# A GpSimd release, six VectorE instructions and a sum moved in the routing step of a mixture of experts

## The reference

```python
probs = softmax(t @ router_w + router_b)
grouped = probs.reshape(-1, N_GROUPS, EXPERTS_PER_GROUP)
group_score = sum(top_k(grouped, 2)[0], axis=-1)
g_sel = argmax(group_score)
top_v, top_i = top_k(where(in_group(g_sel), probs, -1.0), 2)
gates = top_v / sum(top_v, axis=-1)
for e in range(16):
    gu = t @ w_gu[e]
    h = silu(gu[:, :256]) * gu[:, 256:]
    out = out + combine[:, e:e + 1] * (h @ w_down[e])
x = layer_norm(ALPHA * x + out)
```

## Time and profile before

| | us |
|---|---|
| median of three runs | 872.21 (871.42 to 874.04) |
| the profiled execution | 871.15 |
| its span in the profile | 869.4 |
| TensorE busy | 846.3 (97%) |
| VectorE busy | 568.5 (65%) |
| ScalarE busy | 428.1 (49%) |
| GpSimd busy | 128.9 (15%) |

### The profile page before, as it was taken

How to read it: one execution, slowest core, us unless ns; L and a number is a source line. 1 busy time by engine, 2 the same in 40 slices (tenths; PEclk the granted TensorE clock), 3 DMA queues, 4 the chain that set the end, 5 groups by cost and what they waited for, 6 DMA issues and landing times.

```text
span 869.4 us, 10034 instructions
## 1 busy us (share of the span) xinstructions
PE 846.3 (97%) x4026; PEld 684.2 (79%) x4026; DVE 568.5 (65%) x716; ACT 428.1 (49%) x429; POOL 128.9 (15%) x126
## 2 busy tenths in 40 slices
PE   8999999999999999999998999999999999999986
PEld 6888888888888578888864888888888678888853
DVE  4532434456756789999966625425666699999947
ACT  4433222353522388888864131122314388888860
POOL 2400000010400222243220000000000223323210
PEclk9999999999999999999999999999999999999999
DMA  9993313112459399999969432220247599999863
GB/s 344 354 351 97 98 49 96 49 49 98 125 203 374 104 392 346 362 353 345 321 236 383 171 97 98 97 96 1 97 174 311 189 390 349 357 328 355 310 224 146
DMA packets 80835, 193.86 MB, mean 223 GB/s; under 512 B 8249, under 2 KB 8437, under 8 KB 80656
## 3 DMA queue, kind: packets, MB, share of 16 engines
q1 hardware_dynamic: 67344, 159.46, 51.1%
q0 software_dynamic: 13440, 33.69, 10.6%
HBM read 178.95 MB, written 30.43 MB: 241 GB/s over the span
## 4 chain that ended last, share of the span: by engine, by line
PE 88%; DVE 5%; DMA 4%; issue 1%; ACT 1%; SPq 0%; POOL 0%; ACTq 0%; POOLq 0%
PE ps L497 61%; PE ps L878 8%; PE ps L573 3%; PE ps L821 3%; PE ps L647 2%; PE ps L632 2%; DMA expert_out<-arena,rows_of 1%; DMA arena<-expert_out 1%; PE ps L849 1%; PE ps L556 1%; DVE w_lo L1377 1%; PE ps L582 1%; PE ps L736 1%; PE ps L729 1%; PE ps L864 1%
## 5 line engine op out<-in xcount | busy, mean ns | idle before, releaser
L1377 DVE TENSOR_TENSOR w_lo<-arena,w_hi 128x2048 fp32r<-128x2048 f32 x100 | 229.5, 2296 | 125.1 <-ACT w_hi L1062 123.4
L1062 ACT ACTIVATE w_hi<-arena 128x2048 fp32r<-128x2048 f32 x100 | 191.5, 1915 | 158.2 <-PE ps L497 150.6
L497 PE MATMUL ps<-w_hi,xt_hi 128*128 128x512 f32 x480 | 192.4, 401 | 0.0
L497 PE MATMUL ps<-w_hi,xt_lo 128*128 128x512 f32 x480 | 187.4, 390 | 0.0
L497 PE MATMUL ps<-w_lo,xt_hi 128*128 128x512 f32 x480 | 187.1, 390 | 0.0
L497 PE MATMUL ps<-xt_hi,w_hi 128*128 128x512 f32 (+1 forms) x336 | 125.7, 374 | 1.9 <-DVE xt_lo L1385 1.9
L497 PE MATMUL ps<-xt_hi,w_lo 128*128 128x512 f32 (+1 forms) x336 | 124.0, 369 | 0.0
L497 PE MATMUL ps<-xt_lo,w_hi 128*128 128x512 f32 (+1 forms) x336 | 123.9, 369 | 0.0
L497 PEld LDWEIGHTS ps<-w_hi,xt_lo 128*128 128x128 f32 x480 | 90.1, 188 | 19.3
L497 PEld LDWEIGHTS ps<-w_lo,xt_hi 128*128 128x128 f32 x480 | 90.3, 188 | 17.7
L497 PEld LDWEIGHTS ps<-w_hi,xt_hi 128*128 128x128 f32 x480 | 90.2, 188 | 17.5
(11 more groups left out here) (245 smaller groups left out, 1038.1 us busy)
## 6 DMA issues: line engine op xcount, KB each, us to landing
arena<-in_moe_w_gu SPq DMA_DIRECT2D x64, 1024.0 KB, 16.6
arena<-in_moe_w_down SPq DMA_DIRECT2D x32, 1024.0 KB, 17.6
arena<-in_mlstm_w_in SPq DMA_DIRECT2D x16, 1024.0 KB, 6.6
arena<-in_conv_w_in SPq DMA_DIRECT2D x12, 1024.0 KB, 11.6
expert_out<-ln_b POOLq DMA_DIRECT2D x8, 1024.0 KB, 13.8
arena<-expert_out SPq DMA_DIRECT2D x16, 512.0 KB, 7.5
arena<-in_mlstm_w_out SPq DMA_DIRECT2D x4, 1024.0 KB, 5.0
x_of_experts<-arena SPq DMA_DIRECT2D x8, 512.0 KB, 10.3
```

Source lines behind the costliest of these rows:

```text
L497: ins = pe.matmul(out, a, b, start=first and n == 0, stop=last and n == 2)
L1062: act.activation(w_hi[:, parity, :], raw(slot), ACT.Copy).then_inc(s_hi, 1)
L1377: dve.tensor_tensor(w_lo[:, parity, :], raw(slot), w_hi[:, parity, :].bitcast(F32), ALU.subtract).then_inc(s_lo, 1)
```

## The change

Three moves, each made in both layers. On GpSimd the release `s_gi` is raised between the first gather and the second. On VectorE the six instructions of the shares leave `choose` and stand in `experts` between the remainders of the first expert's two weight parts. The sum over places, with its wait for TensorE's second table, stands behind the second of these remainders. TensorE's, ScalarE's and SyncE's programs stay as they are.

```diff
@@ choose
                 step_done(dve.tensor_copy(last_token[:, :], ps[:, 7, 2 * (E - 1):2 * (E - 1) + 1]))
 
+            def shares_by_expert():
+
                 do(dve.tensor_tensor(r_one[:, :], top_value[:, 0, :], top_value[:, 1, :], ALU.add))
                 do(dve.reciprocal(r_one[:, :], r_one[:, :]))
                 do(dve.tensor_tensor(gate_of[:, :, :], top_value[:, :, :],
...
                 by_expert(gates, shares).then_inc(s_gv, 1)
+
+            def slot_gates(layer):
                 dve.wait_ge(s_gm, layer + 1)
                 dve.tensor_reduce(gate_slot[:, :], ps[:, 7, 2 * E:4 * E].rearrange("p (e c) -> p e c", c=2), AX.X,
                                   ALU.add).then_inc(s_gs, 1)
@@ experts, VectorE
                 dve.wait_ge(s_gi, layer + 1)
                 units(0, 0, 0)
+                shares_by_expert()
                 units(0, 0, 1)
+                slot_gates(layer)
                 gathered_lo(0, 0)
@@ experts, GpSimd
-                for e in range(2):
-                    gather(e, e)
+                gather(0, 0)
                 pool.engine_nop().then_inc(s_gi, 1)
+                gather(1, 1)
                 norm_weights(1 + 2 * layer, ln2_g[layer], ln2_b[layer])
```

More of the change, by code:

```diff
@@ L266, in trunk @@
         s_rc = sem("router_weights_centred")
-        s_gi = sem("first_gathers_issued")
+        s_gi = sem("first_gather_issued")
         s_xr = sem("x_tile_ready")
```

## The result

The changed kernel takes 888.63 us, the median of four runs (884.28 to 890.99), against 871.82 us of the kernel before in the same measurement: 1.0174 times as long, with an interval of 1.0129 to 1.0218. Measured again beside the first experiments it took 887.25 us against 871.96, ratio 1.0186 (1.0162 to 1.021). So it is 15 to 17 us slower. I had said slower by 11 to 12, 883.0 us, with a range up to 885.3: the direction and the wait are as forecast, the size is not, because the price of TensorE's lower clock came out at twice what I had put in.

A forecast was written before the change was run, and what follows sets the result against it. The prediction took TensorE, busy 97% of 869.4 us, as the bound. 871.15 us plus 8.50 for the wait and 3.0 for the clock gave 882.65, 883.7 on the median; it said 883.0, range 879.2 to 885.3.

The forecast's parts named there:

- What is late and what is exact: Around the routing stages: the gates have no slack, within 0.2 us; the weight remainders and first gather's landing end no wait.
- Release and order on VectorE: First remainder starts 1.32 us sooner per layer; shares follow it, so gates are ready at 299.58 and 685.42 us.
- What stands behind the wait: On TensorE's queue, table, fillers, transposes and experts' products start 4.30 and 4.20 us later: 8.50 us in all.
- What comes back: In the expert stage, earlier remainders are hidden and worth nothing; up to 2.4 us possible, taken as 0.
- Second gather: Running beside a remainder, it takes likely 1.0 us, at worst 3112 ns; its transposes stay covered, so 0 added.
- TensorE's clock: After idling about 4.2 us per layer TensorE returns at half rate: 1.5 us per layer, 3.0 us for both.
- Rival (a): TensorE's delay without a full double clock fall: none gives 879.7 to 880.7 us, one up to 882.2; chance 0.36.
- (b): VectorE and GpSimd slow each other, by a stretched remainder or later release: 884.3 to 885.6 us; chance 0.07.
- (c): Not slower, as transfers set the expert stage's pace and loads are released sooner: 868.5 to 872.2 us; chance 0.04.
- (d): Release comes when the gather is issued, not worked off; remainder 1.1 us sooner per layer: 877.5 to 881 us; chance 0.05.

The follow-up runs named there:

- shares_first: The changed kernel with the six instructions of the shares back ahead of VectorE's wait, early release and later sum kept: 871.81 us, ratio 0.9994 to the kernel before.
- old_release: The changed kernel with GpSimd's release back behind both gathers, the shares still between the remainders: 891.35 us, ratio 1.0211 to the kernel before.
- fill_wait: The changed kernel with five more calls of fillers ahead of TensorE's wait for the shares: 880.92 us, ratio 1.0115 to the kernel before.
- fill_moved: The changed kernel with five more filler calls ahead of TensorE's wait and the four behind the table taken out: 874.55 us, ratio 1.0019 to the kernel before.
- wide_first: The changed kernel with the four filler calls moved between TensorE's wait and the gates' table: 888.18 us, then 885.03 us measured again.
- table_late: The changed kernel with TensorE's wait and gates' table moved behind the first tile's transposes, six filler calls ahead of these: 872.09 us, ratio 0.9973 to the kernel before.

## Why the prediction was right and where it failed

- What is late and what is exact: right. The gates had no slack and became what TensorE waits for; the remainders were not late, and starting them sooner is worth nothing (shares_first).
- Release and order on VectorE: right within 0.2 us. The remainder starts 1.16 us behind the gather's start, as worked out, and TensorE's table 5.03 us behind it, for 4.90 forecast. The missing tenth is in the six instructions: they took 1.6 us instead of 1.43, the cast (L1788) 0.34 instead of 0.17 us, which it takes only beside the second gather (old_release).
- What stands behind the wait: right. 8.50 us forecast; 8.71 in the profiles of one execution each, 9.0 in the medians with the clock held (fill_wait). That the fillers are issued behind the wait although nothing needs them by then is most of it (fill_moved).
- What comes back: nothing, as forecast, from the expert stage; in the profiles about 1.7 us in the tail of layer 0, which I had not seen, and which the medians do not bear out.
- Second gather: right that it was covered, wrong about the likely case. I had put 1.0 us as likely and 3.1 as the worst; it took 2.94 and 2.95 us. The trace of the kernel before could have told: the one gather of 3.11 us in it started 0.08 us behind a remainder, while those that started about 0.5 us ahead of one took 1.0 us:

```profile
400.00 2.29 DVE L1377 TENSOR_TENSOR w_lo<-arena,w_hi 128x2048 fp32r<-128x2048 f32 x1 [0.24 <-ACT w_hi L1062]
...
400.08 3.11 POOL L2056 DMA_INDIRECT arena<-x_of_experts,rows_of  x1 [0.30 <-issue]
```

- TensorE's clock: the step that failed. The prediction put it as "bounds of 0 and 1.64 us per layer; I take 1.5", 3.0 us for both. Measured are 6.3 us in the medians, and in the profiles 3.1, 3.0 and 3.4 us in the three layers whose slow stretch was long, 1.7 in the one where it was short. I had taken the price from the one slow stretch that began as TensorE came back and had wide matmuls behind it. Here the clock stayed down twice as long in three stretches of four. That the narrow table behind the wait is the reason is likely and not shown (wide_first). The upper bound was a single row, and I treated it as a bound of the mechanism.
- Rival (a), a fall in one layer only, was the wrong way to widen the range: the clock's loss went the other way. (b), (c) and (d) did not occur: the remainder kept its 2.29 us beside the gather and was released behind the first one.
- The measured point: 871.82 + 8.5 + 6.3 = 886.6, where the range ended at 885.3 and the median came at 888.63 and 887.25. The 2.0 us left of the first median are less than the spread of its four runs. The profiled execution, 884.28 us, lies inside the range by luck: it had one short stretch of two, and the shorter tail of layer 0.

## What to carry to other kernels

Before an instruction is moved behind a wait, look at who waits for its result: six small instructions with no slack cost 4.3 to 4.4 us per layer when the wait for a gather and a 2.3 us remainder went ahead of them. Fillers that stand behind a wait in program order are paid after it (6.4 of the 9.0 us here); put them ahead of it. And a gap of TensorE can be paid twice, by its length and by a slow stretch behind it that can be longer than the gap itself (6.8 us behind 4.2, at a cost of 3.1); keep the range of that second price open upward.

## What the runs showed of the hardware that was not expected

- The clock's lower level lasted 3.4 or 6.8 us in the stretches looked at here, up to 3.4 us lost in one. It was also seen at places of routing with hardly any idle time: in shares_first the fillers behind the first table took 3.66 us instead of 1.96, in an execution with no gap ahead of them, and in table_late the clock was down for 6.8 us from about 285.1 us on with TensorE busy throughout. The time of one and the same program moved with it from 867 to 881 us. The Trainium skill, "TensorE: Matmul & The Clock Gate", Part 1, says that the point at which the clock changes is not tied to the start of the kernel and so varies between runs; the runs agree. The same section puts the ramp's penalty under 1% of a typical kernel's span; the 6.6 us here are 0.75% of the span, which agrees, and still nearly half of the change's effect.
- An indirect gather that GpSimd starts 0.23 us behind a VectorE remainder (`tensor_tensor`, both inputs in SBUF, 2.29 us) takes 2.94 us instead of 1.01 and ends 0.88 us after it. Gathers that start about 0.5 us ahead of such a remainder take their usual 1.00 to 1.03 (steady expert steps of the kernel before). The remainder itself keeps its 2.29 us, but a cast of 128 x 8 beside the held gather takes 0.34 us instead of 0.17.
